# Moving small vector work of a decoder step from VectorE to GpSimd, and one GpSimd operation behind VectorE's norm

## The reference, cut to what matters

```python
h = rmsnorm(x, g_pre_ffn)                       # before the dense feed-forward
f = (silu(h @ wg) * (h @ wu)) @ wd              # dense, width 2816
x = x + rmsnorm(f, g_post_ffn)
kv = rmsnorm(x, g_kv) @ w_kv                    # shared K and V
...                                             # attention, then in layer 1:
top_p, top_i = top_k(softmax(h @ w_router + b_router), 2)
gates = sum(one_hot(top_i, 8) * (top_p / sum(top_p))[..., None], axis=-2)
for e in range(8):                              # experts of width 1408
    y = y + gates[..., e:e+1] * swiglu(h, wg[e], wu[e], wd[e])
y_out = x + rmsnorm(y, g_post_ffn)
```

## Time and profile before

| | us |
|---|---|
| median of 3 runs | 1826.3 |
| the profiled execution | 1821.79 |
| its span | 1820.0 |
| PE busy | 1693.2 (93%) |
| DVE busy | 943.6 (52%) |
| ACT busy | 745.8 (41%) |
| POOL busy | 539.9 (30%) |
| mean granted TensorE clock | 0.957 of full |

### The profile page before, as it was taken

The page is one execution under the profiler, slowest core; times in us unless marked ns, Lnnn a source line. Parts: engine busy times, 40 slices in busy tenths (PEclk is TensorE's granted clock), DMA queues, the critical chain, the costliest instruction groups (busy, mean ns, idle before and its releaser), DMA issues.

```text
span 1820.0 us, 29086 instructions
## 1 busy us (share of the span) xinstructions
PE 1693.2 (93%) x11312; PEld 1537.1 (84%) x11312; DVE 943.6 (52%) x1161; ACT 745.8 (41%) x977; POOL 539.9 (30%) x326
## 2 busy tenths in 40 slices
PE   6898797999999998989898998899999999999988
PEld 5898687999999997889666486899898988989886
DVE  6796534211111001322486423877686776868686
ACT  6354453322222122321355222554454554545454
POOL 1001223355554444242000021352331524324161
PEclk8899888999999999999898999899999999999989
DMA  6623202144445342121532415579799796977961
GB/s 206 123 85 131 70 24 70 47 144 144 144 144 181 103 144 86 47 93 60 193 129 84 151 59 130 175 249 297 205 268 232 227 273 208 290 207 237 252 238 49
DMA packets 346267, 281.96 MB, mean 155 GB/s; under 512 B 9505, under 2 KB 311117, under 8 KB 346055
## 3 DMA queue, kind: packets, MB, share of 16 engines
q1 hardware_dynamic: 324947, 251.09, 47.3%
q10 hardware_dynamic: 18084, 18.14, 3.0%
q0 software_dynamic: 3168, 11.80, 2.1%
HBM read 246.62 MB, written 35.10 MB: 155 GB/s over the span
## 4 chain that ended last, share of the span: by engine, by line
PE 77%; DVE 12%; ACT 5%; issue 3%; DMA 1%; SPq 1%; POOL 1%; ACTq 0%; DVEq 0%; POOLq 0%
PE ps L2331 34%; PE ps L2871 14%; PE ps L2874 6%; PE ps L2317 3%; PE ps L2319 2%; PE ps L2318 2%; PE ps L2898 2%; PE ps L2897 2%; DVE cT L1606 2%; PE ps L2459 2%; DVE wlo L1483 1%; PE ps L2293 1%; PE ps L2283 1%; PE ps L2356 1%; DVE zc L1924 1%
## 5 line engine op out<-in xcount | busy, mean ns | idle before, releaser
L2871 PE MATMUL ps<-ejx,ewh 128*128 128x384 f32 x1408 | 403.0, 360 | 5.5 <-DVE ejx L2114 3.6
L2100 DVE TENSOR_TENSOR ewl<-eraw,ewh 128x2048 fp32r<-128x2048 f32 (+1 forms) x144 | 304.0, 2111 | 156.4 <-ACT ewh L1325 156.3
L1325 ACT ACTIVATE ewh<-eraw 128x2048 fp32r<-128x2048 f32 (+1 forms) x144 | 255.2, 1773 | 259.6 <-PE ps L2874 152.8
L2874 PE MATMUL ps<-ejx,ewl 128*128 128x192 f32 x1408 | 353.1, 251 | 0.0
L2331 PE MATMUL ps<-hh,whi 128*128 128x260 f32 x1504 | 315.5, 292 | 31.8 <-DVE hl L1838 25.0
L2331 PE MATMUL ps<-hh,wlo 128*128 128x260 f32 x1504 | 308.8, 288 | 0.0
L2331 PE MATMUL ps<-hl,whi 128*128 128x260 f32 x1504 | 308.5, 287 | 0.0
L867 POOL TENSOR_TENSOR ea<-eat,ea 128x128 fp32r<-128x128 f32 x88 | 176.3, 2003 | 378.5 <-ACT ea L1383 378.4
L2871 PEld LDWEIGHTS ps<-ejx,ewh 128*128 128x128 f32 x1408 | 265.2, 188 | 8.8 <-issue 8.8
L2331 PEld LDWEIGHTS ps<-hh,whi 128*128 128x128 f32 x1504 | 240.3, 194 | 35.4 <-issue 24.8
L2874 PEld LDWEIGHTS ps<-ejx,ewl 128*128 128x128 f32 x1408 | 269.8, 192 | 0.0
(11 more groups left out here) (437 smaller groups left out, 2627.3 us busy)
## 6 DMA issues: line engine op xcount, KB each, us to landing
eraw<-in_w_gate_e SPq DMA_DIRECT2D x88, 512.0 KB, 4.8
eraw<-in_w_up_e SPq DMA_DIRECT2D x88, 512.0 KB, 6.2
eraw<-in_w_down_e SPq DMA_DIRECT2D x64, 512.0 KB, 6.0
eraw<-in_w_down_e SPq DMA_DIRECT2D x48, 256.0 KB, 2.8
xs<-zero ACTq DMA_DIRECT2D x10, 1152.0 KB, 4.8
raw<-in_w_gate_d SPq DMA_DIRECT2D x22, 512.0 KB, 4.0
raw<-in_w_up_d SPq DMA_DIRECT2D x22, 512.0 KB, 5.2
raw<-in_w_down_d SPq DMA_DIRECT2D x16, 512.0 KB, 4.5
```

The costliest lines, as they stand in the source:

```text
L1325: e.activation(ewh[:, s, 0:n], eraw[:, u % RAW, 0:n], ACT.Copy).then_inc(ew_hi, 1)
L2100: e.tensor_tensor(ewl[:, s, 0:n], eraw[:, u % RAW, 0:n], ewh[:, s, 0:n].bitcast(F32), ALU.subtract)\
L2871: e.matmul(ps[:, q, 0:2 * C], ewh[:, s, o:o + P], ejx[:, k, :, :].rearrange("p h n -> p (h n)"), start=(k == 0), stop=(k == KD - 1), skip_ ...
L2874: ins = e.matmul(ps[:, q, C:2 * C], ewl[:, s, o:o + P], ejx[:, k, 0, :], start=False, stop=(k == KD - 1), skip_group_check=True)
```

## The change

Four edits:

- GpSimd waits for all eight low parts of the norm (`n_lo`) before it computes the low part of the second chunk, at both dense places.
- `row_out(0)` moves on VectorE up to where the count is awaited. `row_out(1)` moves behind `expert_lo(0, 1)`. So the rows of tile 0 are scattered earlier and `htok` of tile 1 comes later.
- In the last job the slot arithmetic (three operations on `tle` and the one that writes `sle`) and the last three of the gates (`inl`, `gme`, `gate_last`) go from VectorE to GpSimd, each with a wait for its own end. What stays on VectorE is in `gates(0)` to `gates(6)`, behind the steps 2 to 8. `last_ready` is raised to 1 by GpSimd behind `gate_last`, and ScalarE and TensorE wait for that; TensorE waits for the one-hot matrices (`oh`) by itself. GpSimd's row reads wait for `sle` by order.
- The residual sums of row tiles 0 and 2 are done by GpSimd, behind everything else in its program; SyncE's stores wait for them.

```diff
@@ SyncE
-            for i in range(NT):
-                e.wait_ge(f_dve, FD[f"out{i}"])
+            for i in (0, 1, 2, 3):
+                if i in (0, 2):
+                    e.wait_ge(f_pool, i // 2 + 1)
+                else:
+                    e.wait_ge(f_dve, FD[f"out{i}"])
@@ GpSimd
+            e.wait_ge(n_lo, KD)
             with e.Fori(0, KF // 2) as i:
                 for j in range(2):
                     lo_of_at(U_GU + j + 1, i, 2)
...
+            e.wait_ge(n_lo, 2 * KD)
             with e.Fori(0, 3) as i:
                 for j in range(2):
                     lo_of_at(U_KV + j + 1, i, 2)
...
+            def step(ins):
+
+                steps[0] += 1
+                ins.then_inc(last_step, 1)
+                e.wait_ge(last_step, steps[0])
+
+            step(e.tensor_tensor(out=tle[:, :, :], in0=own_slot[:, :].unsqueeze(1).to_broadcast([P, 2, NT + 1]), in1=slf[:, :, :],
+                                 op=ALU.subtract))
+            e.wait_ge(f_dve, FD["inl"])
+            step(e.tensor_tensor(out=tle[:, :, :], in0=tle[:, :, :], in1=inl[:, :, :], op=ALU.mult))
+            step(e.tensor_tensor(out=tle[:, :, :], in0=tle[:, :, :], in1=slf[:, :, :], op=ALU.add))
+            step(e.tensor_scalar(sle[:, :, :], tle[:, :, :], float(C), None, ALU.add))
             for m in range(KE):
+                if m == 6:
+                    e.wait_ge(f_dve, FD["gate1"])
+                    step(e.tensor_tensor(out=inl[:, :, :], in0=gate[:, :, :], in1=inl[:, :, :], op=ALU.mult))
+                    step(e.tensor_tensor(out=gme[:, :, :], in0=gate[:, :, :], in1=inl[:, :, :], op=ALU.subtract))
+                    e.tensor_tensor(out=gate_last, in0=inl[:, 0, :], in1=inl[:, 1, :], op=ALU.add).then_inc(last_ready, 1)
...
+            for i in (0, 2):
+                e.wait_ge(f_dve, FD[f"w{i}"])
+                e.tensor_tensor(out=fw[:, i, :], in0=fw[:, i, :], in1=xtk[:, i, :], op=ALU.add).then_inc(f_pool, 1)
@@ ScalarE, early_one
-                    e.wait_ge(last_ready, 2)
+                    e.wait_ge(last_ready, 1)
@@ VectorE
             row_low(0)
+            e.wait_ge(gf_in, 16)
+            row_out(0)
...
-                    if last and 1 <= u <= 9:
-                        last_rows(u - 1)
+                    if last and 2 <= u <= 8:
+                        gates(u - 2)
...
             expert_lo(0, 0)
-            e.wait_ge(gf_in, 16)
-            row_out(0)
-            row_out(1)
...
             expert_lo(0, 1)
+            row_out(1)
             row_out(2)
...
-                e.tensor_tensor(fw[0:n, i, :], fw[0:n, i, :], xtk[0:n, i, :], ALU.add).then_inc(f_dve, 1)
+                if i not in (0, 2):
+                    e.tensor_tensor(fw[0:n, i, :], fw[0:n, i, :], xtk[0:n, i, :], ALU.add).then_inc(f_dve, 1)
@@ TensorE, selection
-                e.wait_ge(last_ready, 2)
+                e.wait_ge(last_ready, 1)
+                e.wait_ge(f_dve, FD["oh"])
```

More of the change, by code:

```diff
@@ L376, in build @@
         yr_in = [sem(f"yr_in{i}") for i in range(NT + 1)]
-        gp_in, f_act, f_dve, f_pe = map(sem, "gp_in f_act f_dve f_pe".split())
+        last_step, gp_in, f_act, f_dve, f_pe, f_pool = map(sem, "last_step gp_in f_act f_dve f_pe f_pool".split())
         def counts(names):
@@ L383, in build @@
                     "y0 y1 y2 y3 hi4 sq0 root0 sq1 root1 sq2 root2 sq3 root3 sq4 root4")
-        FD = counts("sum0 sum1 sum2 sum3 lo0 lo1 lo2 lo3 sum4 y0 y1 y2 y3 lo4 "
-                    "inv0 w0 out0 inv1 w1 out1 inv2 w2 out2 inv3 w3 out3 inv4 w4 out4")
+        FD = counts("inl gate0 gate1 oh sum0 sum1 sum2 sum3 lo0 lo1 lo2 lo3 sum4 y0 y1 y2 y3 lo4 "
+                    "inv0 w0 inv1 w1 out1 inv2 w2 inv3 w3 out3 inv4 w4 out4")
         F_BANKS = [0, 6, 2, 4, 0]
@@ L883, in _ @@
                     rest(j, m)
-            for m in range(KE):
+            steps = [0]
+            def step(ins):
[8 more added lines that the diff above has]
+            step(e.tensor_scalar(sle[:, :, :], tle[:, :, :], float(C), None, ALU.add))
+            for m in range(KE):
+                if m == 6:
[3 more added lines that the diff above has]
+                    e.tensor_tensor(out=gate_last, in0=inl[:, 0, :], in1=inl[:, 1, :], op=ALU.add).then_inc(last_ready, 1)
                 if m == 3:
@@ L888, in _ @@
                     e.wait_ge(xs_in, 160)
-                    e.wait_ge(last_ready, 1)
                 if m == KE - 1:
@@ L2151, in early_lo, with gates @@
                                 ALU.subtract).then_inc(f_dve, 1)
-            def last_rows(part):
-                if part == 2:
-                    e.wait_ge(rr_act, RR_EXP)
+            def gates(part):
                 if part == 0:
                     link(e.tensor_scalar(lbase, jobf[:, MAXJOBS:MAXJOBS + 1], float(C), -float(C), ALU.mult, ALU.add))
[L2159 to L2166, removed]
+                    e.tensor_scalar(inl[:, :, :], slf[:, :, :], lbase, None, ALU.is_ge).then_inc(f_dve, 1)
+                    e.wait_ge(rr_act, RR_EXP)
                     link(e.tensor_reduce(zs, pr, AX, ALU.add))
@@ L2169, in last_rows @@
                     link(e.tensor_tensor(pr, pr, over_e(zs), ALU.mult))
+                if part == 1:
                     link(e.tensor_tensor(dl, pr, oh1, ALU.mult))
-                if part == 3:
                     link(e.tensor_reduce(p1, dl, AX, ALU.add))
                     link(e.tensor_tensor(dl, pr, oh2, ALU.mult))
+                if part == 2:
                     link(e.tensor_reduce(p2, dl, AX, ALU.add))
                     link(e.scalar_tensor_tensor(out=pp, in0=p1, scalar=1e-30, in1=p2, op0=ALU.max, op1=ALU.add))
-                if part == 4:
                     link(e.reciprocal(pp, pp))
[L2178 to L2183, removed]
+                if part == 3:
+                    e.tensor_tensor(gate[:, 0, :], p1, pp, ALU.mult).then_inc(f_dve, 1)
+                    e.tensor_tensor(gate[:, 1, :], p2, pp, ALU.mult).then_inc(f_dve, 1)
                     link(e.tensor_tensor(own_last, slf[:, 0, :], slf[:, 1, :], ALU.max))
                     link(e.tensor_scalar(own_last, own_last, lbase, None, ALU.subtract))
-                if part >= 6:
-                    for i in ((0, 1), (2, 3), (4,))[part - 6]:
+                if part >= 4:
+                    for i in ((0, 1), (2, 3), (4,))[part - 4]:
                         n = P if i < NT else B
@@ L2192, in last_rows @@
                                                   ALU.is_equal)
-                if part == 8:
-                    ins.then_inc(last_ready, 1)
+                if part == 6:
+                    ins.then_inc(f_dve, 1)
             def expert_dve(j, first=False, last=False):
```

## The result

The changed kernel takes **1809.39 us** (median of four runs, 1808.62 to 1812.53) against 1826.37 for the kernel before beside it (four runs): the ratio is 0.9912, with an interval of 0.9900 to 0.9924. It is 17.0 us faster (13.9 to 18.3 by the interval). 1808.8 was forecast, in a range of 1804.5 to 1816.

The account below looks back on a forecast made before the run. TensorE, busy for 93% of the span, was taken as the bound, so only its gaps could give time. 8.5 + 1.8 + 4.6 + 2.3 + 0.3 = 17.5 us off 1826.3 gave 1808.8 us, range 1804.5 to 1816.

Parts of the forecast that it names:

- The last job: TensorE's 4.89 us gap ahead of the last job's `selection` nearly closes with small operations on GpSimd: 4.6 us.
- Norms: Both dense norms: VectorE's 5.00 us operation takes 0.75, so TensorE starts 4.25 us sooner in each: 8.5 us.
- Router and first job: Ahead of the first job: two `row_out` operations leave the way to `ejx`, 1.8 us of their 2.47 gained.
- the margin of 0.6 us: Last job: GpSimd's later three operations were to finish at 1753.7, 0.6 us ahead of `ewl` of step 11.
- rival 1: Last job: GpSimd misses the gap ahead of `ewl` of step 11, gaining 1.7 us there; 1814.0 us, chance 0.28.
- The clock of the one-column products: Last job: without the gap the twenty products run at the high clock, half of 4.59 us: 2.3 us gained.
- The end: Last row tiles: GpSimd takes two sums, VectorE's others wait for it; a pair costs 5.1 instead of 5.3: 0.3 us.
- Rivals 3 and 4: 3: norm's gain hidden at second chunk, 1818.2 us, chance 0.08. 4: GpSimd's last-job operations blocked, 1834.6 us, chance 0.04.
- The prediction's 1 to 3.25 us: GpSimd's DMA preparations last that long beside VectorE; given as an argument for GpSimd missing the last job's gap.

Follow-up runs that it names:

- e1: The kernel before with only GpSimd's two waits on `n_lo` in the norms; 1814.99 us, ratio 0.9939.
- g4: The changed kernel itself, unedited, run once more as the measure for its group; 1808.53 us, ratio 0.9912.
- h2: The changed kernel, but GpSimd's subtractions in the norms wait only for each norm's first low part, not the eighth; 1819.93 us, ratio 0.9972.
- g2: The changed kernel with one more `n_lo` wait: GpSimd's subtraction ahead of the query projection goes behind VectorE's low parts; 1802.32 us, ratio 0.9875.
- e2: The kernel before with only the scatter rows (`row_out(0)`, `row_out(1)`) moved; 1825.54 us, ratio 0.9996.
- h3: The changed kernel without the scatter-row edit: both `row_out` back ahead of `ejx`; 1811.32 us, ratio 0.9921.
- g1: The changed kernel with GpSimd's last three slot operations behind row 5 instead of row 6 of the last job but one; 1806.88 us, ratio 0.9888.
- g3: The changed kernel with GpSimd's first job written out and its last two `htok` scatters between that job's row copies; 1808.59 us, ratio 0.9907.
- h1: The changed kernel with both the row-5 slot operations and the third `n_lo` wait at the query projection; 1798.72 us, ratio 0.9858.
- e4: The kernel before with only the residual sums of row tiles 0 and 2 on GpSimd; 1825.50 us, ratio 0.9995.
- h4: The changed kernel without the edit at the end: VectorE forms all five residual sums again; 1811.72 us, ratio 0.9923.

## Why the prediction was right, and where it was not

The time came out at 1809.39 for a forecast of 1808.8, and so close partly by luck. The last job and the clock of its products gave 4.1 us less than their terms, and the clock behind the norms, which had no term, gave 2.6 us in the changed kernel's profile and 4.1 in e1's and g4's.

1. **Norms, 8.5 us.** The mechanism is shown: GpSimd's subtraction stops VectorE's operation with two SBUF operands (e1, h2, g2). The gap itself gave 7.9 us in the profiles. Alone the edit gave 11.2, since TensorE's clock stays up in stretches behind it, 4.1 us in e1's profile. I had charged the clock only to the last job. In the changed kernel's profile two of e1's three faster stretches are there (1.5 and 1.1 us), in g4's all three. h2 keeps the last of them without the norm's gain, so only the other two can follow from the closed gaps, and the second comes and goes between executions.
2. **Router and first job, 1.8 us.** 1.6 by the profile, gap of 1.89 us as forecast; 0.7 by the median of e2, which is not clear of noise. The gap alone is no proof, as kernels without the edit show 1.89 us too when TensorE's products ahead of it ran slower (h3).
3. **The last job, 4.6 us: mis-sized, 2.8 in the profile.** The step that failed is the margin of 0.6 us. The sixth row read ended 0.85 us ahead of `ewl` of step 11, where I had worked out 1.5. The first two operations took 0.6 us with their waits, as forecast. The third would have needed 0.3 more; it started 0.2 us ahead of `ewl` and ended with it. The sum also took the start of `ewl` as the limit, where `eat`, 0.27 us ahead of it, reads two SBUF operands too; that `eat` was what held the third operation is likely from the rows, but no run separates the two. That is rival 1, with a smaller price than its 2.9 us, since two of the three operations were already done: ScalarE went on at 1747.04, and the gap was 2.1 us and not 3.1. g1 gives 1.9 us of it back by moving three operations one row ahead.
4. **The clock of the one-column products, 2.3 us: nothing.** They took 2.18 and 2.38 us, as before (2.21 and 2.38). The price was too high for the twenty products (1.8 between g3 and the changed kernel) and too low for the whole low stretch (3.0). The step that failed is the assumption that the level follows from the gap. It was high over all twenty behind gaps of 1.29 us (g3, h2) and none (h1), over the first ten only behind 0.17 (g1) and 2.13 (h3), and low from the first ten on behind 2.09 (changed kernel, g4) and 4.89 (before). What decides is open.
5. **The end, 0.3 us.** The pair of tiles costs 4.97 us instead of 5.3 (first `fw` to third, 1793.47 to 1798.44), and the whole end is 0.72 shorter, of which the later first `fw` takes 0.38 back. VectorE's sums of tiles 1 and 3 took 2.02 and 1.98 us and GpSimd's 2.40, as forecast. By medians 0.7 (e4) to about 3 (h4): too small to settle.
6. **Rivals 3 and 4** did not happen. No gap stood ahead of the second chunk. VectorE never waited for `rest` in the last job's first steps: GpSimd's slot operations there took 0.21 to 0.29 us, in VectorE's pauses.

## What to carry to other kernels

When GpSimd and VectorE both work in SBUF, look for single operations of VectorE that last several times their kin, and move GpSimd's large one behind the stretch that TensorE waits for; then look for every other place of the same form, edited or not. Here a small operation on GpSimd took 0.25 us in a pause of VectorE and 2.5 just ahead of a large one, so issue such operations a whole step early rather than with a margin of half a us. And a gap that closes may give more than its length, in TensorE's clock behind it: price that as a bound, not as a term, since here it came in some executions and not in others.

## What the runs showed of the hardware

- An indirect DMA's preparation on GpSimd took 0.95 us at its shortest for 128 rows and up to 4.29 beside VectorE's two-operand subtractions and `htok` (4.28 in h3). The prediction's 1 to 3.25 us is the last job's; the first job of the kernel before already has one of 4.29, at 1179.92.
- The clock of TensorE fell or stayed behind the same gap of 2.28 us in the norm: granted 0.89 over 330 to 345 us in before, 1.00 in the changed kernel, 0.89 in h2. What differed is TensorE's idle time some 20 us earlier, 9.81 us, 5.57, or 5.57 and 3.21. That alone does not decide it: the second norm has 5.57 and 2.28 us in nine profiled executions, and in the 15 us behind it the clock was 1.00 in five of them (e1, g3, g4, h3, h4) and 0.89 in four (the changed kernel, g1, g2, h1). At the first norm it was 1.00 in all nine, and with 9.8 us it was 0.89 at both norms in all four kernels that have it.
- VectorE's sum of two SBUF operands, started 0.93 us before GpSimd's own sum of 2.40 us ended, took 2.02 us instead of 1.23 and ended 1.1 us behind it: read from the rows, its work was held until GpSimd's was done, and then ran at about its pace. The Trainium skill, SBUF — State Buffer, section "Who interferes with whom", says that the later of the two waits for the shared ports; the trace agrees, 1797.24 (GpSimd's end) + 1.09 us = 1798.33.
